# Sixteen modulation chunks of layer 1 move from layer 0's attention into layer 1's own stages

## The chip, the cores and the metric

One core of one Trainium2 chip runs the whole kernel in one launch. The metric is the device time in microseconds; three runs of the kernel before gave 1990.22, 1991.87 and 1993.07 us, and 1991.87 is their median. Engines are called by their names in the profile: PE is TensorE (PEld its weight loads), DVE VectorE, ACT ScalarE, POOL GpSimd, and SP the engine that issues most DMAs.

## The reference, cut to what matters

Two blocks run one after the other on 256 tokens of width 1024 (and 256 context tokens). The first block has two layers. Each computes, for a vector c and for the context's vector:

```
mod = silu(c) @ w_mod[l] + b_mod[l]            # 6 * 1024 values
sh1, sc1, gt1, sh2, sc2, gt2 = split(mod, 6)
proj = (rms_norm(x, g1) * (1 + sc1) + sh1) @ w_in
o_mla, o_gqa = attention(proj), attention(proj);  o_four = fourier_mix(proj)
x = x + gt1 * merge_branches(o_mla, o_gqa, o_four, gates)
x = x + gt2 * conv_ffn(rms_norm(x, g2) * (1 + sc2) + sh2)
```

sh1 and sc1 are wanted at the start of a layer, the other four from its merge on. Layer 0 also updates the context (four tiles of 128 rows, queries of the two context tiles see 256 keys, the others 512); layer 1 updates only the two token tiles, all with 512 keys. The second block (another mixer pair) is not touched.

## The kernel before, in words

Every engine has its program written out by hand; they meet by semaphores that count up. Products are made from two or three passes over split values (coarse and fine parts). Weights come through a ring of RING = 2 raw slots in SBUF, filled by SP in one fixed order (`load`, `chunks`, `stream`; L2898 is its DMA), each slot after the user of its last content has released it. For most weights ACT makes the coarse part (L1137) and DVE the fine one (L1839) before PE multiplies.

The modulation is cut into chunks of 256 columns, 24 for each layer. A chunk takes one raw slot (1 MB of w_mod) and is used unsplit: `mod_product` (L538) multiplies its eight rows of blocks in four strips of a bank, DVE copies the 98 rows out (`mod_row`, L1891), PE turns them with two transposes (L474), and DVE adds the strips and the bias into `mod_t` (L1871, L1872). `mod_chunk` of each engine does the second half of the chunk before and the first half of the next. The first eight chunks of layer 0 are made at the start. The other 16 of layer 0 and all 24 of layer 1 are made in layer 0: one in each of the eight tiles of `heads_prep`, and 32 in the attention's `heads_loop`, at the heads i listed in MOD_FILLS, which are the odd ones; `mod_chunk(last=True)` finishes the last one.

In `heads_prep`, for each tile PE makes the next tile's latent products (L527), then the chunk, then the transposes of the heads (L474); ACT squares and takes roots, DVE sums, scales and rotates (L2063 to L2088 for rotated tiles), and the transposes wait for it. In `heads_loop` the turn i has the score of head i (L693), the transposes of the exponentials of head i - 2 (L700), on even i the products with the values for heads i - 4 and i - 3 (L710), and then the fill. DVE takes the maximum (L2164, L2167), ACT the exp (L1402) and the copy of the turned exponentials (L1411), for which L710 waits.

Then `fourier` (L741, L751) runs over four groups for each pair of tiles, eight in layer 0 and four in layer 1. In its turn j = 2, in layer 0, `gate_transposes` turns the gate values (gt1 and gt2) of both layers into rows, and DVE's `other_gains` copies them out (L1821) to `gate_rows`, makes the three mod_gain products that are left (L1907) and raises mod_ready to 2. POOL waits for that, writes the rows to DRAM (L2818) and waits until they have landed; it reads them back, spread over partitions, for the merge's end and the FFN's end of each layer (L2825). ACT waits for the same landing ahead of `merge`, since its sigmoids (L1460) go to a buffer that lies over `gate_rows`; ACT's splits of the merge's weights stand behind that wait. In `merge` each slot carries 18 blocks of weights, the first slot is split during `fourier`, the second one inside the merge.

Of the kernel before, what the change touches and what calls it, by code (L numbers as in the profile page):

```python
# [13 lines left out]
P = 128  # L14
D = 1024
KD = D // P
SEQ = 256
DEPTH = 2
# [66 lines left out]
MOD_FILLS = [16 * t + i for t in range(4) for i in range(1, 16, 2)]  # L85
# [116 lines left out]
def two_block_kernel(nc, a, out):  # L202
    ctx = ExitStack()
    with ctx:
# [101 lines left out]
        gate_rows = rows(2 * KD, X + 17024, 512)  # L306
# [102 lines left out]
        def _(pe):  # L409
# [157 lines left out]
            def mod_chunk(last=False):  # L567

                if mod_copied:
                    pe.wait_ge(bank_read[mod_copied[-1][0]], mod_copied[-1][1])  # L570
                    transposes([mod_row[:, m * P:(m + 1) * P] for m in range(2)], parts_in=MOD_ROWS)
                if not last:
# [61 lines left out]
            def heads_prep(l):  # L634
# [18 lines left out]
                for s, (kind, t) in enumerate(tiles):  # L653
                    copied = following
                    if s + 1 < len(tiles):
                        following = products(*tiles[s + 1])
                    if l == 0:
                        mod_chunk()
                    mla_transposes(kind, t, raw[s % 2], copied)
                    gqa_transposes(kind, t)  # L660

            def attend(l):
# [17 lines left out]
                heads_loop(16 * items_of(l), score, value, pr, prT, keys_of, exp_done, mod_chunk, MOD_FILLS if l == 0 else (), sums_t)  # L680
# [39 lines left out]
            def gate_transposes(reads):  # L720

                evacuated(reads)
                ps = begin()
                for l in range(DEPTH):
                    for use, sec in enumerate((2, 5)):
                        blk = mod_t[:, l, sec * KD:(sec + 1) * KD, :].rearrange("p k s -> p (k s)")
                        j = 2 * l + use
                        mm = nc.tensor.transpose(ps[0:2 * KD, j * P:(j + 1) * P], blk, ident[:, :])
                end(mm)
# [142 lines left out]
            for l in range(DEPTH):  # L872
                norm(4, project=True, started=int(l == 0))
                project(l)
                latents(l)
                heads_prep(l)
                attend(l)
                if l == 0:
                    mod_chunk(last=True)
                    reads = list(u.reads)  # L880
                fourier(l, (lambda: gate_transposes(reads)) if l == 0 else None)
                merge(l)
                mix_out(l)
                norm(items_of(l))
                ffn_up(l)
                ffn_down(l)
# [194 lines left out]
        def _(act):  # L1081
# [74 lines left out]
            def mod_chunk(last=False):  # L1156
                if mod_chunks[0]:
                    skip()
                if not last:
                    ring.next()  # L1160
                    skip()
                    mod_chunks[0] += 1
# [20 lines left out]
            def norm(l, second, nt, updates):  # L1183
# [5 lines left out]
                act.wait_ge(mod_ready, 1 if l == second == 0 else 2)  # L1189
# [102 lines left out]
            def heads_prep(l):  # L1292
# [75 lines left out]
                for s, (kind, t) in enumerate(tiles):  # L1368
# [4 lines left out]
                    if l == 0:  # L1373
                        mod_chunk()
# [3 lines left out]
            def attend(l):  # L1378
# [3 lines left out]
                def after(g, b, n):  # L1382
# [5 lines left out]
                           MOD_FILLS if l == 0 else (), after, True)  # L1388
# [54 lines left out]
            def merge(l):  # L1443
                n = items_of(l) * P
                act.wait_ge(gates_saved, 16)
# [94 lines left out]
            for l in range(DEPTH):  # L1540
# [6 lines left out]
                if l == 0:  # L1547
                    mod_chunk(last=True)
                fourier(l, skip if l == 0 else None)
# [225 lines left out]
        def _(dve):  # L1775
# [98 lines left out]
            filled, noted = [FIRST_MOD], [FIRST_MOD]  # L1874

            def mod_units(last=False):

                units = [later()] if noted[0] > FIRST_MOD else []
                noted[0] += 1
                return units if last else units + [later()]  # L1880

            def mod_chunk(units=None, last=False):

                units = units or mod_units(last)
                if filled[0] > FIRST_MOD:
                    mod_out(units[0], *divmod(filled[0] - 1, MOD_CHUNKS), 1)
                if not last:
# [5 lines left out]
            def other_gains(reads):  # L1893

                copy_out(gate_rows, 2 * KD)
# [146 lines left out]
            def heads_prep(l):  # L2042
# [54 lines left out]
                for s, (kind, t) in enumerate(tiles):  # L2097
# [4 lines left out]
                    chunk = mod_units() if l == 0 else None  # L2102
# [30 lines left out]
                    if chunk:  # L2133
                        mod_chunk(chunk)
# [3 lines left out]
            def attend(l):  # L2138
                def after(g, b, ps):
                    if g >= 2:  # L2140
# [4 lines left out]
                           mod_chunk, MOD_FILLS if l == 0 else (), after, True)  # L2145
# [230 lines left out]
            for l in range(DEPTH):  # L2376
# [7 lines left out]
                if l == 0:  # L2384
                    mod_chunk(last=True)
                    reads = list(u.reads)
                fourier(l, (lambda: other_gains(reads)) if l == 0 else None)
# [324 lines left out]
        def _(pool):  # L2712
# [66 lines left out]
            for l in range(DEPTH):  # L2779
# [36 lines left out]
                if l == 0:  # L2816
# [65 lines left out]
        def _(sp):  # L2882
# [48 lines left out]
            for l in range(DEPTH):  # L2931
# [7 lines left out]
                if l == 0:  # L2939
# [114 lines left out]
```

## Time and profile before

| what | value |
|---|---|
| median of 3 runs | 1991.87 us |
| span of the profiled execution | 1988.9 us |
| PE busy | 1877.4 us (94%) |
| DVE, ACT, POOL busy | 1162.5, 933.1, 198.5 us |
| mean granted clock of PE | 0.983 |
| w_mod DMAs | 48 of 1024 KB |
| layer 0: preparation from its first chunk, attention, Fourier | from 151.9, 198.0, 342.1 us |
| layer 1: attention, Fourier, merge | from 1081.3, 1160.0, 1169.7 us |

The profiled execution has no other time than its span, from the first to the last instruction; the median of the timed runs is 3.0 us above it. The stage times are starts of PE's instructions in the timeline. A busy PE counts its pipelined matmuls to their modelled ends, so it can show as fully busy where the next matmul merely follows without a wait.

### The profile page before, as it was taken

Reading aid. Unit: us, or ns where it says so; the run is one execution under the profiler, and the core shown is the slowest. Engines: PE = TensorE matmul, PEld = TensorE weight load, DVE = VectorE, ACT = ScalarE, POOL = GpSimd, SP = SyncE. Lnnn points to the kernel's source line nnn. Section 1 sums busy time; section 2 is a strip of 40 time slices with the busy share of each in tenths; the row PEclk is TensorE's granted clock in tenths of the full one; section 3 lists DMA queues with packets and bytes.
Section 4 is the critical chain, followed back from the end, with each engine's and each line's share of the span. In section 5 each row is a group of like instructions: output and inputs, shape, how many; then the busy total and the mean of one; then the engine's idle time right before and its main releaser. Section 6 shows DMA issues by size and latency. Waiting matters only on the chain.

```text
span 1988.9 us, 31268 instructions
## 1 busy us (share of the span) xinstructions
PE 1877.4 (94%) x12063; PEld 1571.9 (79%) x12063; DVE 1162.5 (58%) x1802; ACT 933.1 (47%) x1427; POOL 198.5 (10%) x203
## 2 busy tenths in 40 slices
PE   5999999999998999999998889989999999899997
PEld 2875565788887888888784579989989888799996
DVE  3326566444346555523535456677744578789987
ACT  3327555323324333311436654455534656387782
POOL 4010001000011223210100000023301000100000
PEclk9999999999998999999998999989999999999999
DMA  9225668333332232232250036645557433444442
GB/s 310 91 80 169 197 221 273 97 95 95 90 110 81 89 102 94 96 116 95 85 170 6 1 88 177 191 143 181 178 190 217 158 118 104 150 151 146 146 137 101
DMA packets 262855, 265.36 MB, mean 133 GB/s; under 512 B 6342, under 2 KB 230960, under 8 KB 262752
## 3 DMA queue, kind: packets, MB, share of 16 engines
q1 hardware_dynamic: 257856, 249.32, 40.4%
q0 software_dynamic: 4448, 13.49, 2.2%
q8 instruction: 71, 1.16, 0.3%
q10 hardware_dynamic: 448, 1.12, 0.2%
q14 instruction: 32, 0.26, 0.0%
HBM read 262.81 MB, written 1.10 MB: 133 GB/s over the span
## 4 chain that ended last, share of the span: by engine, by line
PE 78%; DVE 12%; ACT 5%; DMA 2%; issue 2%; SPq 0%; DVEq 0%; ACTq 0%
PE bank L480 21%; PE bank L481 21%; PE bank L482 21%; PE bank L693 4%; DVE weights_fine L1839 2%; PE bank L710 2%; DMA region<-in_w_mod 2%; PE bank L538 2%; PE bank L474 2%; PE bank L527 2%; PE bank L700 1%; ACT weights_coarse L1137 1%; DVE region L2482 1%; DVE small L2164 1%; PE bank L950 0%
## 5 line engine op out<-in xcount | busy, mean ns | idle before, releaser
L1839 DVE TENSOR_TENSOR weights_fine<-region,weights_coarse 128x2048 fp32r<-128x2048 f32 (+2 forms) x181 | 417.7, 2308 | 346.8 <-ACT weights_coarse L1137 345.7
L1137 ACT CAST weights_coarse<-region 128x2048 fp32r<-128x2048 f32 (+3 forms) x185 | 355.0, 1919 | 333.0 <-PE bank L482 323.9
L480 PE MATMUL bank<-normed_coarse,weights_coarse 128*128 128x256 f32 (+1 forms) x1104 | 371.3, 336 | 9.2 <-DVE normed_fine L1977 4.3
L481 PE MATMUL bank<-normed_fine,weights_coarse 128*128 128x256 f32 (+1 forms) x1104 | 370.9, 336 | 0.0
L482 PE MATMUL bank<-normed_coarse,weights_fine 128*128 128x256 f32 (+1 forms) x1104 | 370.8, 336 | 0.0
L480 PEld LDWEIGHTS bank<-normed_coarse,weights_coarse 128*128 128x128 f32 x1104 | 212.4, 192 | 30.7 <-issue 10.1
L481 PEld LDWEIGHTS bank<-normed_fine,weights_coarse 128*128 128x128 f32 x1104 | 212.3, 192 | 20.5
L482 PEld LDWEIGHTS bank<-normed_coarse,weights_fine 128*128 128x128 f32 x1104 | 212.3, 192 | 20.4
L480 PE MATMUL bank<-x_turned_coarse,weights_coarse 128*128 128x256 f32 x616 | 177.8, 289 | 8.7 <-DVE weights_fine L1839 4.2
L481 PE MATMUL bank<-x_turned_fine,weights_coarse 128*128 128x256 f32 x616 | 175.5, 285 | 0.0
L482 PE MATMUL bank<-x_turned_coarse,weights_fine 128*128 128x256 f32 x616 | 175.5, 285 | 0.0
L1479 ACT ACTIVATE region<-bank,cols 128x512 f32<-128x512 f32 (+1 forms) x88 | 59.1, 672 | 216.4 <-PE bank L482 216.4
L480 PEld LDWEIGHTS bank<-x_turned_coarse,weights_coarse 128*128 128x128 f32 x616 | 119.4, 194 | 12.5 <-DVE weights_fine L1839 5.4
L2277 DVE SCALAR_TENSOR_TENSOR region<-bank,cols,region 128x510 f32<-128x510 f32 (+1 forms) x88 | 54.0, 614 | 114.0 <-ACT region L1479 113.0
L481 PEld LDWEIGHTS bank<-x_turned_fine,weights_coarse 128*128 128x128 f32 x616 | 119.5, 194 | 0.0
L482 PEld LDWEIGHTS bank<-x_turned_coarse,weights_fine 128*128 128x128 f32 x616 | 119.4, 194 | 0.0
L1402 ACT ACTIVATE region<-bank,small,q_scale 128x512 f32<-128x512 f32 (+1 forms) x96 | 67.9, 707 | 95.6 <-DVE small L2167 91.4
L693 PE MATMUL bank<-region 96*128 96x512 f32 (+4 forms) x224 | 106.6, 563 | 3.6 <-ACT region L1353 1.5
L480 PE MATMUL bank<-weights_coarse,ffn_mid_coarse 128*128 128x512 f32 x264 | 102.8, 389 | 0.9 <-DVE region L2243 0.9
L481 PE MATMUL bank<-weights_fine,ffn_mid_coarse 128*128 128x512 f32 x264 | 102.7, 389 | 0.0
L482 PE MATMUL bank<-weights_coarse,ffn_mid_fine 128*128 128x512 f32 x264 | 102.7, 389 | 0.0
L474 PE MATMUL bank<-ident,region 128*128 128x128 f32 (+3 forms) x449 | 69.0, 285 | 32.9 <-DMA ident<-in_c_ident 7.6
(295 smaller groups left out, 3574.4 us busy)
## 6 DMA issues: line engine op xcount, KB each, us to landing
region<-in_w_mod SPq DMA_DIRECT2D x48, 1024.0 KB, 5.3
region<-in_w_up SPq DMA_DIRECT2D x44, 1024.0 KB, 5.1
region<-in_w_in_c SPq DMA_DIRECT2D x30, 1024.0 KB, 5.2
region<-in_w_in_ab SPq DMA_DIRECT2D x20, 1024.0 KB, 5.3
region<-in_w_in SPq DMA_DIRECT2D x32, 512.0 KB, 4.7
region<-in_w_down SPq DMA_DIRECT2D x16, 1024.0 KB, 5.0
region<-in_w_in SPq DMA_DIRECT2D x14, 1024.0 KB, 5.0
region<-in_w_in SPq DMA_DIRECT2D x16, 384.0 KB, 3.5
```

Source lines behind the costliest of these rows:

```text
L474: mm = nc.tensor.transpose(ps[0:w, j * width:j * width + parts_in], blk, ident[0:parts_in, 0:parts_in])
L480: nc.tensor.matmul(o, sc, mc, start=first, stop=False)
L481: nc.tensor.matmul(o, sc, mf, start=False, stop=False)
L482: return nc.tensor.matmul(o, sf, mc, start=False, stop=last)
L527: mm = nc.tensor.matmul(ps[:, 0:n], acts[:, k, t * P:(t + 1) * P], w[:, k, c0:c0 + n], start=(k == 0), stop=(k == k_rows - 1))
L538: mm = nc.tensor.matmul(ps[strip:strip + 2, 0:COLS], sil_c[:, k, :], w[:, k, :], start=(k < MOD_STRIPS), stop=(k >= KD - MOD_STRIPS))
L693: nc.tensor.matmul(pb[4 + J % 2][:, 0:keys_of(i)[1] * P], q, k, start=True, stop=True).then_inc(scores_done, 1)
L1137: nc.scalar.copy(w_co[:, p, 0:size], raw_w[:, s, 0:size]).then_inc(coarse_ready, 1)
L1402: nc.scalar.activation(p_sb[:, J % 2, 0:nk], src, ACT.Exp, bias=small[:, at + J % 4:at + 1 + J % 4], scale=q_scale[:, i // 16, i % 16:i % ...
L1479: nc.scalar.activation(acc[:, j, 0:n], ps[:, 0:n], ACT.Identity, scale=cols[:, 2 * l, bass.ds(c + T_TAP1, 1)], bias=cols[:, 2 * l + 1, bas ...
L1839: nc.vector.tensor_tensor(w_fi[:, p, 0:size], raw_w[:, s, 0:size], w_co[:, p, 0:size].bitcast(F32), ALU.subtract).then_inc(fine_ready, 1)
L2277: link(nc.vector.scalar_tensor_tensor(out=a_s[:, :, 1:SEQ], in0=u_s[:, :, 0:SEQ - 1], scalar=cols[:, 2 * l, bass.ds(f + T_TAP0, 1)], in1=a ...
```

## The change

MOD_FILLS becomes a list for each layer. Layer 0's attention keeps 16 fills (the heads 1, 5, 9, 13 of each of its four tiles), which with the eight of its preparation finish layer 0 and make the first eight chunks of layer 1 (sh1 and sc1). Layer 1's other 16 chunks are made in layer 1: six in its preparation, ten in its attention. SP's order of loads follows. The gate transposes, the gate rows, their write to DRAM and the waits for it are done once in each layer, each for its own layer; mod_gain is made for layer 0's second norm and layer 1's first in layer 0, and for layer 1's second norm in layer 1. The number of chunks stays 48. The core of the diff:

```diff
-MOD_FILLS = [16 * t + i for t in range(4) for i in range(1, 16, 2)]
+MOD_FILLS = [[16 * t + i for t in range(4) for i in range(1, 16, 4)],
+             [16 * t + i for t in range(2) for i in (1, 5, 7, 11, 13)]]
...
-        gate_rows = rows(2 * KD, X + 17024, 512)
+        gate_rows = rows(2 * KD, X + 17024, 2 * P)
...  PE, ACT and DVE, heads_prep
-                    if l == 0:
-                        mod_chunk()
+                    mod_chunk()
...
-            def gate_transposes(reads):
+            def gate_transposes(l, reads):
 
                 evacuated(reads)
                 ps = begin()
-                for l in range(DEPTH):
-                    for use, sec in enumerate((2, 5)):
+                for use, sec in enumerate((2, 5)):
...  PE, ACT and DVE, the layers' loop
-                if l == 0:
-                    mod_chunk(last=True)
-                    reads = list(u.reads)
-                fourier(l, (lambda: gate_transposes(reads)) if l == 0 else None)
+                mod_chunk(last=True)
+                reads = list(u.reads)
+                fourier(l, lambda: gate_transposes(l, reads))
...  ACT
-                act.wait_ge(mod_ready, 1 if l == second == 0 else 2)
+                act.wait_ge(mod_ready, 1 if l == second == 0 else 2 + l * second)
...
-                act.wait_ge(gates_saved, 16)
+                act.wait_ge(gates_saved, 16 * (l + 1))
...  DVE
-            def other_gains(reads):
+            def other_gains(l, reads):
 
-                copy_out(gate_rows, 2 * KD)
+                copy_out(gate_rows, 2 * KD, 2 * P)
...
-                for layer, second in ((0, 1), (1, 0)):
-                    step(gains(layer, second))
-                gains(1, 1).then_inc(mod_ready, 1)
+                if l < DEPTH - 1:
+                    step(gains(l + 1, 0))
+                gains(l, 1).then_inc(mod_ready, 1)
...  POOL
-                if l == 0:
-                    pool.wait_ge(mod_ready, 2)
-                    pool.dma_start(gate_dram.rearrange("c r n -> r c n"),
-                                   gate_rows.rearrange("r (c n) -> r c n", c=2 * DEPTH)).then_inc(gates_saved, 16)
-                    pool.wait_ge(gates_saved, 16)
+                pool.wait_ge(mod_ready, l + 2)
+                pool.dma_start(gate_dram[2 * l:2 * l + 2].rearrange("c r n -> r c n"),
+                               gate_rows.rearrange("r (c n) -> r c n", c=2)).then_inc(gates_saved, 16)
+                pool.wait_ge(gates_saved, 16 * (l + 1))
...  SP
-                if l == 0:
-                    chunks(w_mod[0], FIRST_MOD * COLS, MOD)
-                    for later in range(1, DEPTH):
-                        chunks(w_mod[later], 0, MOD)
+                chunks(w_mod[l], FIRST_MOD * COLS, MOD)
+                if l < DEPTH - 1:
+                    chunks(w_mod[l + 1], 0, FIRST_MOD * COLS)
```

## Rows read from the trace of the kernel before

**Rows 1.** The page: its span, and the chain that ended last by engine.

```profile
span 1988.9 us, 31268 instructions
...
PE 78%; DVE 12%; ACT 5%; DMA 2%; issue 2%; SPq 0%; DVEq 0%; ACTq 0%
```

**Rows 2.** Waits of PE, layer 0's attention: us in total, times, longest.

```profile
PE bank L538 <- DMA region<-in_w_mod: 1.0, 2, 0.6
```

**Rows 3.** Timeline of PE, layer 0's attention, 512 keys: start, duration, instructions, [idle before].

```profile
220.93 0.33 PE L474 MATMUL bank<-ident,region 98*128 98x98 f32 x2
...
222.17 1.12 PE L693 MATMUL bank<-region 128*128 128x512 f32 x2
```

**Rows 4.** Timeline of PE, layer 1's attention.

```profile
1105.45 1.09 PE L710 MATMUL bank<-region 128*64 128x128 f32 x16 [0.62 <-ACT region L1411]
```

**Rows 5.** Timeline of PE, the end of layer 0's attention, 256 keys.

```profile
333.53 0.70 PE L693 MATMUL bank<-region 128*128 128x256 f32 x2
...
336.37 0.66 PE L710 MATMUL bank<-region 128*64 128x128 f32 x8
336.96 0.70 PE L693 MATMUL bank<-region 128*128 128x256 f32 x2
...
339.32 0.66 PE L710 MATMUL bank<-region 128*64 128x128 f32 x8
```

**Rows 6.** Timeline, head preparation of layer 0 and of layer 1.

```profile
154.81 1.19 PE L474 MATMUL bank<-ident,region 128*96 128x128 f32 x9 [1.90 <-DVE region L2129]
...
178.48 1.51 PE L474 MATMUL bank<-ident,region 128*96 128x128 f32 x12
...
183.27 0.42 DVE L2088 TENSOR_TENSOR region<-region 128x256 f32<-128x256 f32 x1
...
1052.95 1.19 PE L474 MATMUL bank<-ident,region 128*96 128x128 f32 x9 [2.84 <-DVE region L2129]
...
1072.44 1.04 PE L474 MATMUL bank<-ident,region 128*96 128x128 f32 x8
...
1078.88 1.11 PE L474 MATMUL bank<-ident,region 128*128 128x128 f32 x4 [0.92 <-DVE region L2088]
...
1081.26 3.78 PE L693 MATMUL bank<-region 96*128 96x512 f32 x4 [1.27 <-ACT region L1351]
```

**Rows 7.** Windows: busy time of each engine, then PEclk, DMA share and GB/s.

```profile
198.60:201.80 3.20, 3.20 (x9) 1.15 (x10) 1.01 (x3) 1.52 (x3) 0.77 (x1) 0.52 0.20 44
1079.00:1089.00 10.00, 8.48 (x16) 3.82 (x17) 2.55 (x6) 4.86 (x9) 0.74 (x1) 0.50 0.11 28
978.00:983.20 5.20, 5.20 (x25) 5.20 (x26) 4.42 (x9) 1.43 (x4) 0.00 (x0) 0.50 0.31 126
```

**Rows 8.** Timeline of layer 0's Fourier stage, and DMA issues (KB, us to landing).

```profile
342.06 1.93 PE L741 MATMUL bank<-region 128*128 128x258 f32 x8
...
351.54 0.67 DVE L1821 COPY region<-bank 16x512 f32<-16x512 f32 x1
...
352.98 0.54 POOL L2818 DMA_DIRECT2D gate_rows<-region  x1 [8.20 <-DVE mod_gain L1907]
...
gate_rows<-region POOLq DMA_DIRECT2D x1, 32.0 KB, 4.7
...
out<-x_tok SPq DMA_DIRECT2D x4, 256.0 KB, 2.1
```

**Rows 9.** Timeline of layer 1's Fourier stage and the merge's first turn.

```profile
1160.04 1.91 PE L741 MATMUL bank<-region 128*128 128x258 f32 x8
...
1167.52 1.28 ACT L1137 ACT_TABLE_LOAD   x1
1168.82 2.12 ACT L1137 CAST weights_coarse<-region 128x2304 fp32r<-128x2304 f32 x1
...
1171.87 2.55 DVE L1839 TENSOR_TENSOR weights_fine<-region,weights_coarse 128x2304 fp32r<-128x2304 f32 x1
...
1177.78 0.28 PE L480 MATMUL bank<-normed_coarse,weights_coarse 128*128 128x256 f32 x1
```

More of the change, by code:

```diff
@@ L571, in mod_chunk @@
                     transposes([mod_row[:, m * P:(m + 1) * P] for m in range(2)], parts_in=MOD_ROWS)
-                if not last:
+                if last:
+                    mod_copied.clear()
+                else:
                     mod_product()
@@ L678, in value @@
                     return proj[:, kt, at:at + 64]
[L680 removed]
+                heads_loop(16 * items_of(l), score, value, pr, prT, keys_of, exp_done, mod_chunk, MOD_FILLS[l], sums_t)
             def heads_loop(heads, score, value, p_sb, pT_sb, keys_of, scores_read, fill, fills, sums):
@@ L1158, in mod_chunk @@
                     skip()
+                mod_chunks[0] = int(not last)
                 if not last:
@@ L1372, in heads_prep @@
                         squares_of(s + 1)
-                    if l == 0:
-                        mod_chunk()
+                    mod_chunk()
                     turned_mla(kind, t)
@@ L1546, in _ @@
                 attend(l)
-                if l == 0:
-                    mod_chunk(last=True)
-                fourier(l, skip if l == 0 else None)
+                mod_chunk(last=True)
+                fourier(l, skip)
                 merge(l)
@@ L1872, in mod_out @@
                 read(nc.vector.tensor_tensor(mod_t[:, l, at, :], mod_t[:, l, at, :], bias, ALU.add), b)
-            filled, noted = [FIRST_MOD], [FIRST_MOD]
+            filled, noted = [FIRST_MOD, False], [False]
             def mod_units(last=False):
-                units = [later()] if noted[0] > FIRST_MOD else []
-                noted[0] += 1
+                units = [later()] if noted[0] else []
+                noted[0] = not last
                 return units if last else units + [later()]
@@ L1884, in mod_chunk @@
                 units = units or mod_units(last)
-                if filled[0] > FIRST_MOD:
+                if filled[1]:
                     mod_out(units[0], *divmod(filled[0] - 1, MOD_CHUNKS), 1)
+                filled[1] = not last
                 if not last:
@@ L2101, in heads_prep @@
                         skip(2)
-                    chunk = mod_units() if l == 0 else None
+                    chunk = mod_units()
                     skip(2)
@@ L2132, in heads_prep @@
                         nc.vector.tensor_tensor(keys, src, over_heads(small[:, 72:74], GQA_KV, GQA_DIM), ALU.mult).then_inc(gqa_ready, 1)
-                    if chunk:
-                        mod_chunk(chunk)
+                    mod_chunk(chunk)
                     before = turning
@@ L2144, in attend @@
                 heads_loop(16 * items_of(l), lambda i: 512 if i < 32 else 256, o_raw, sums_t, None,
-                           mod_chunk, MOD_FILLS if l == 0 else (), after, True)
+                           mod_chunk, MOD_FILLS[l], after, True)
             def heads_loop(heads, keys_of, raw_o, sums, bias, fill, fills, after, scaled=False):
@@ L2383, in _ @@
                 attend(l)
[L2384 to L2387, printed above, removed]
+                mod_chunk(last=True)
+                reads = list(u.reads)
+                fourier(l, lambda: other_gains(l, reads))
                 merge(l)
```

10 lines of the change are left out of this document (3 added, 7 removed).

## The prediction

> **What bounds the kernel now.** I began with the page's span and its chain of waits: TensorE carries 78% of the chain [rows 1]. Only gaps and extra work on TensorE therefore count, and I read the timeline in the stages that the change touches. Layer 0's attention is full: each turn with a modulation chunk shows no wait between the operations of TensorE, so each chunk pushes the rest back [rows 3], and twice the chunk's DMA was late as well, 1.0 us in all [rows 2]. Layer 1's attention has no chunks and waits 0.62 us per pair of heads for ScalarE's copy [rows 4]. Layer 1's head preparation waits at its first tile (2.84 us) and at its last two stages (0.92 and 1.27 us) [rows 6]. The windows of the granted clock show 10 us at 0.50 (1.2 of 2.4 GHz) from the end of that preparation into the attention, and only 3.2 us at the same place of layer 0 [rows 7].
>
> **Out of layer 0's attention** go 16 of 32 fills, at i = 3, 7, 11, 15 of each tile. A fill is two transposes and 16 matmul records: 220.93 to 222.17 is 1.24 us [rows 3]. While heads have 512 keys (8 of the 16), its place becomes a wait of 0.62 us, as in layer 1 [rows 4]: 8 x (1.24 - 0.62) = 5.0 us.
> With 256 keys the trace has no pair without a fill, so I bound it. From the odd head's score (336.96) to the product that needs the copy behind it (339.32) the chain score, maximum, exp, copy takes 2.36 us [rows 5]. In a pair with a fill TensorE comes to that product only after 336.37 - 333.53 = 2.84 us [rows 5], so nothing waits. Without the fill it would come at 2.84 - 1.24 = 1.60 us and wait until 2.36: a fill is worth 2.84 - 2.36 = 0.48. The bounds are 0 (another engine paces) and 1.24 (no wait). The last fill (i = 63) is worth nothing: its product already stood at 2.36. So 7 x 0.48 = 3.4 us. Half the chunks also halve the stream from HBM, and the 1.0 us of late DMAs goes [rows 2]. Sum 9.4 us.
>
> **Layer 0's Fourier stage** keeps its gate transposes, for one layer: the copy of the gate rows is 16x256 where it was 16x512 (0.67 us, [rows 8]), some 0.25 us less, and one gain product of three goes. TensorE waits for that copy's bank; I take 0.3 us. Sum for layer 0: 9.7 us saved.
>
> **Into layer 1's head preparation** go 6 chunks. I follow layer 0, which has the same first five tiles with chunks. From the first to the fifth set of MLA transposes layer 0 takes 178.48 - 154.81 = 23.67 us, layer 1 takes 1072.44 - 1052.95 = 19.49 [rows 6]: +4.18. The first tile's chunk falls into the 2.84 us wait and is free. The last tile is paced by VectorE's rotation, not by TensorE: in layer 0 the last rotate of the sixth tile ends at 183.27 + 0.42 = 183.69, the transposes behind it could start at 183.75, and layer 1 needs 1081.26 - 1078.88 = 2.38 us from there to its first score [rows 6]. That is 183.75 + 2.38 - 178.48 = 7.65 us from the fifth set on, against 1081.26 - 1072.44 = 8.82 now: -1.17, because the next tile's sums begin earlier against TensorE. Preparation: +3.0 us. Six full chunks (7.4) and 2 are the ends.
>
> **Into layer 1's attention** go 10 fills at odd i, the last at 29. Nine stand in the steady turns at 1.24 - 0.62 = 0.62 us: 5.6 us. The one at i = 1 stands in the stretch at the low clock. Its own price is 1.24; with chunks at the end of the preparation TensorE has fewer gaps, and the cold stretch should come nearer layer 0's 3.2 us than 10 [rows 7]. Half the clock for 6.8 us less is at most 3.4; I take half of it, 1.7, so this place gives -0.5. The ends are -2.2 (all 3.4) and +1.9 (no shorter, and the chunk itself half hidden at twice its price).
>
> The Trainium skill, TensorE: Matmul & The Clock Gate, section "HAM oscillation — how this bites in real kernels", says that gaps in TensorE's work put its clock to half rate and that each return is paid again, so that keeping it fed pays. Here the trace agrees in kind, 0.50 after gaps [rows 7]. It speaks for layer 1 as the home of the chunks; carried through, it is the first rival.
>
> **The seam behind layer 1's attention** is new. SP now puts w_mod chunks ahead of the first merge weights, which had been in their slots since the projection. They are loaded once the fills at i = 27 and 29 are done, with three pairs of heads still to come before the Fourier stage; in layer 0 the last fill has none behind it, and nothing waits for the weights there: hidden. The closing mod_chunk adds two transposes, 0.2 us.
> Then ScalarE may not enter the merge before the gate rows of its own layer are in DRAM, since the sigmoids write over them. Behind that wait on ScalarE stand the split of the second weight slot, VectorE's half of it, and then TensorE. I count from the stage's first matmul (342.06 in layer 0, 1160.04 in layer 1). In layer 0 the copy starts at +9.48, POOL's DMA at +10.92, and it lands 4.7 us later [rows 8]. In layer 1 the same order holds up to there (both wait for ScalarE's 2304-wide split and VectorE's); a narrower copy and one gain instead of three give +10.5, landing +15.2. Table load 1.28, cast 2.12, VectorE 2.55 [rows 9] bring TensorE's second slot to +21.3. It starts at 1177.78, +17.74, now [rows 9]. That is 3.6 us, 3.8 with the transposes. TensorE comes to it about when it does now, so it stands still for 3 us or more; layer 0 hides the same chain because it has eight Fourier groups, not four. The ends: the shortest write to DRAM in the trace lands in 2.1 us [rows 8], which makes it 1.2; a landing two microseconds later than layer 0's makes it 6.
> Cold stretches behind gaps of TensorE are 3.2 us long in the short kind and 5.2 in the longer [rows 7]; half of that is lost, 1.6 or 2.6 us. I take 1.7; 0 and 2.6 are the ends. Layer 1's merge waits for nothing that could give this back.
> DMA: Bandwidth & Descriptors of the Trainium skill, section "Anatomy of one DMA — SWDGE (gpsimd) path", has some 2 us fixed for such a DMA. The trace has 4.7 with the weights' stream running beside it; by the page's figure the seam would cost about 1.1 and hardly any cold time. The measured one stands in the sum.
> POOL has only the gate loads behind its two waits, and these wait for the merge's end anyway. The norms' wait on mod_ready is met long before.
>
> **Sum.** Layer 1: 3.0 + 5.6 - 0.5 + 3.8 + 1.7 = 13.6 us. Layer 0: -9.7. Net +3.9 us. On the profiled span of 1988.9 us that is 1992.8; the median of the runs is 1991.87, 3.0 above that span, so I forecast 1995.8 us. A change of 0.2%, 4.0 us, is about what can be told from none; the forecast lies on that line.
>
> **Rivals.**
> Fed TensorE (the other side). Chunks close the gaps at the end of the preparation, the attention starts in a short cold stretch or none (another 1.7 us back) and the stall in the merge brings no cold time (1.7 less): +3.9 - 3.4 = +0.5, 1992.4, not slower by what can be told. For it: layer 0's 3.2 us. Against it: the rotation still paces the last tile, and TensorE keeps gaps there. It decides once the cold stretch at the start of the attention falls to layer 0's length and the merge stays at full clock.
> Short gate write. It lands in 2.1 us as the output's writes do [rows 8], 2.6 sooner, and the merge's stall is too short for a cold stretch: +3.9 - 2.6 - 1.7 = -0.4, 1991.5. Against it: SP's four issues of the next slot stand at the same place in both layers.
> Colder still. The cold stretch stays at 10 us with the chunk of i = 1 in it (+1.9 for -0.5), and the stall is paid with 5.2 us at half: +3.9 + 2.4 + 0.9 = +7.2, 1999.1.
> The saving does not come. Another engine paces layer 0's 256-key heads, and the late DMAs were part of the same wait: 4.4 us less saved, 2000.2. Against it: in the tail of that attention, with the fill out of the way, the chain itself took 2.36 us [rows 5].
>
> **How the numbers follow.** Forecast 0.56, with its own range 1993.3 to 1998.3; fed TensorE 0.16; short write 0.11; colder 0.11; no saving 0.06. Slower by over 0.2% (above 1995.9): half the forecast's case and the last two: 0.45. Faster by over 0.2% (below 1987.9) needs the first two rivals together and more: 0.07. Within: 0.48. The range that takes in the rivals' centres: 1989.8 to 2000.4.
>
> **What would show it.** Sixteen fills with 0.48 to 0.62 us waits in place of them in layer 0; a pair without fill at 256 keys lasting 2.95 us; layer 1's first score 3.0 us later against the first tile; a table load on ScalarE about 15 us after layer 1's first Fourier matmul, released by the gate write; a TensorE gap of 3 to 5 us before the second slot and 0.50 clock after it. I am wrong if the gate write lands before +12, if the cold stretch before the attention is gone, or if layer 0's pairs keep their length.

## The result and the profile after

The changed kernel takes 2002.26 us in the median of five runs (2001.82 to 2003.16), the kernel before 1991.93 (1990.22 to 1993.07, five runs of the same job). The ratio is 1.0043, with a 95% interval of 1.0031 to 1.0056: 8.6 us slower (6.2 to 11.2 by the interval, which holds the 10.3 us between the two medians). In a later job the changed kernel took 2003.13 and the ratio was 1.0037 (1.0020 to 1.0054). The forecast was 1995.8 with a range up to 2000.4, so it is outside, on the slow side.

The page of the profiled run (2003.16 us, span 2001.3) has the same chain as before [rows 1]:

```profile
span 2001.3 us, 31252 instructions
...
PE 79%; DVE 12%; ACT 5%; issue 2%; DMA 2%; SPq 0%; DVEq 0%; ACTq 0%
```

The difference must be read by stage. The table has the length of each stretch, from one TensorE start to the next, less the same stretch of the profile before; a plus is time lost. "Seam" is layer 1's Fourier stage and merge, up to the output mix; "behind" is all that follows, where the change alters no instruction. The last two columns are a second profile of the changed kernel and one of the kernel before.

| stretch, us | forecast | changed | changed again | before again |
|---|---|---|---|---|
| layer 0 attention | -9.4 | -7.71 | -8.70 | -0.52 |
| layer 0 Fourier | -0.3 | +0.28 | -0.36 | +1.32 |
| layer 1 preparation | +3.0 | +3.21 | +3.21 | 0.00 |
| layer 1 attention | +5.1 | +4.83 | +4.83 | 0.00 |
| layer 1 seam | +5.5 | +7.06 | +7.02 | -0.01 |
| behind | 0 | +4.39 | +4.40 | +0.06 |

**Layer 0's attention.** The timeline of TensorE at the end of it (start, duration, instructions, [idle before]), which answers to [rows 5]:

```profile
326.36 0.66 PE L712 MATMUL bank<-region 128*64 128x128 f32 x8 [0.95 <-ACT region L1409]
...
329.79 0.66 PE L712 MATMUL bank<-region 128*64 128x128 f32 x8
...
332.74 0.66 PE L712 MATMUL bank<-region 128*64 128x128 f32 x8 [0.94 <-ACT region L1409]
```

A pair with a fill lasts 329.79 - 326.36 = 3.43 us, one without 332.74 - 329.79 = 2.95, which is the length forecast. At 512 keys the wait in place of a fill is 0.62, as forecast:

```profile
219.24 1.09 PE L712 MATMUL bank<-region 128*64 128x128 f32 x16 [0.62 <-ACT region L1409]
```

The waits of TensorE in this attention hold no late w_mod chunk any more [rows 2]; ScalarE's copy took its place (us in total, times, longest):

```profile
PE bank L712 <- ACT region L1409: 12.5, 17, 1.0
```

What is missing from the 9.4 us is at the end. Windows of the changed kernel, first the end of layer 0's attention, then the start of layer 1's, which was 10 us at 0.50 [rows 7] (busy time of PE, PEld, DVE, ACT, POOL, then PEclk, DMA share, GB/s):

```profile
334.00:338.50 4.50, 4.28 (x21) 3.62 (x22) 1.53 (x5) 1.10 (x3) 0.70 (x1) 0.62 0.10 24
...
1077.50:1082.00 4.50, 4.50 (x22) 1.48 (x22) 1.95 (x6) 2.69 (x5) 0.75 (x1) 0.62 0.21 59
```

The second window holds about 3.4 us of half clock (4.50 us at 0.62), as much as layer 0's start of attention has [rows 7]. The second profile of the same kernel has the first of these windows at full clock, and there the attention saves 8.70:

```profile
334.00:338.50 4.50, 4.36 (x28) 3.60 (x26) 1.10 (x4) 3.00 (x4) 1.27 (x1) 1.00 0.02 4
```

**The seam.** All engines, layer 1's Fourier stage and the merge's first turn, in the changed kernel; it answers to [rows 9]. The first Fourier matmul starts at 1161.02:

```profile
1168.02 2.55 DVE L1836 TENSOR_TENSOR weights_fine<-region,weights_coarse 128x2304 fp32r<-128x2304 f32 x1
...
1170.49 0.41 DVE L1818 COPY region<-bank 16x256 f32<-16x256 f32 x1
...
1170.60 2.24 SPq L2893 DMA_DIRECT2D region<-in_w_in  x3
...
1171.58 0.55 POOL L2813 DMA_DIRECT2D gate_rows<-region  x1 [7.84 <-DVE mod_gain L1905]
...
1176.81 1.28 ACT L1136 ACT_TABLE_LOAD   x1 [5.88 <-DMA gate_rows<-region]
...
1178.10 2.11 ACT L1136 CAST weights_coarse<-region 128x2304 fp32r<-128x2304 f32 x1
...
1180.25 2.56 DVE L1836 TENSOR_TENSOR weights_fine<-region,weights_coarse 128x2304 fp32r<-128x2304 f32 x1 [6.57 <-ACT weights_coarse L1136]
...
1182.94 0.58 PE L481 MATMUL bank<-normed_coarse,weights_coarse 128*128 128x256 f32 x1 [5.97 <-DVE weights_fine L1836]
...
1187.97 0.28 PE L481 MATMUL bank<-branch_out,weights_coarse 128*128 128x256 f32 x1
```

VectorE's half of the first slot is done, its buffer is free, and SP sends three DMAs for the next slot; 0.98 us behind them POOL sends the 16 KB of gate rows. The write starts at +10.56 (forecast +10.5), the table load at +15.8 (+15.2), and TensorE takes up the work behind the second slot's split at +21.92 (+21.3). It stood still for 5.97 us and then ran at half clock:

```profile
1180.50:1188.00 7.50, 5.06 (x25) 5.07 (x26) 3.54 (x2) 3.79 (x4) 0.00 (x0) 0.54 0.59 151
```

To say how much later that is, the same matmul must be found in the kernel before. In `merge` the wait for the second slot stands behind the first two gates, that is behind 2 x 8 blocks or 48 matmuls, since the third gate takes its blocks from both slots. Windows of the first 48 matmuls of the merge, before and changed:

```profile
1169.70:1177.05 7.35, 7.34 (x48) 7.34 (x49) 4.58 (x9) 2.90 (x3) 0.00 (x0) 0.77 0.83 204
```

```profile
1170.94:1177.00 6.06, 6.01 (x48) 5.81 (x48) 2.43 (x9) 0.19 (x1) 0.55 (x1) 1.00 0.77 197
```

So the 49th is the one to compare, and before it ran at 1177.06, +17.02; the 1177.78 (+17.74) of [rows 9] is the 55th, six matmuls behind the wait. TensorE of the kernel before:

```profile
1177.06 0.28 PE L480 MATMUL bank<-normed_coarse,weights_coarse 128*128 128x256 f32 x1
...
1179.94 0.28 PE L480 MATMUL bank<-branch_out,weights_coarse 128*128 128x256 f32 x1
```

The wait therefore costs 21.92 - 17.02 = 4.90 us. From there to the first matmul on the branches the same 24 matmuls take 1187.97 - 1182.94 = 5.03 us, mostly at half clock, where they took 1179.94 - 1177.06 = 2.88, so 2.15 us go to the clock. The two make up the seam's 7.06.

**Behind the seam.** Windows from the first matmul of layer 1's output mix to the end, before and changed:

```profile
1274.98:1988.90 713.92, 675.42 (x5106) 626.58 (x5104) 531.80 (x724) 406.77 (x538) 65.14 (x66) 0.98 0.48 153
```

```profile
1283.02:2001.30 718.28, 679.21 (x5106) 630.74 (x5104) 532.47 (x724) 407.16 (x538) 65.19 (x66) 0.98 0.47 152
```

The same 5106 matmuls keep TensorE busy for 3.79 us longer, and its waits grow by only 0.57: what is lost there is mostly clock, not waiting. The clearest place is the second block, where nothing was changed. TensorE waits 2.80 us for the same split of weights in both kernels. The kernel before, timeline and window:

```profile
1633.17 0.39 PE L480 MATMUL bank<-x_turned_coarse,weights_coarse 128*128 128x256 f32 x1 [2.80 <-DVE weights_fine L1839]
```

```profile
1633.00:1639.00 6.00, 5.83 (x48) 5.83 (x49) 6.00 (x11) 3.81 (x5) 0.00 (x0) 1.00 0.58 175
```

The changed kernel:

```profile
1642.49 0.58 PE L481 MATMUL bank<-x_turned_coarse,weights_coarse 128*128 128x256 f32 x1 [2.80 <-DVE weights_fine L1836]
```

```profile
1642.40:1649.00 6.60, 6.51 (x32) 6.51 (x33) 6.60 (x11) 3.83 (x5) 0.00 (x0) 0.54 0.54 159
```

The gap is equal; the clock behind it is 2.4 GHz in one and mostly 1.2 in the other. That stretch, from the second block's attention to its mix, is 2.59 us longer, in both profiles of the changed kernel.

### The profile page after: what moved, and what is told of

It is laid out like the page before. It is cut to its first block, busy times and chain, and to the rows that moved or that the text cites. A ratio compares the mean times of both kernels' runs of the same rounds, so it can differ in the third digit from the quotient of the medians.

```text
span 2001.3 us, 31252 instructions
## 1 busy us (share of the span) xinstructions
PE 1883.8 (94%) x12063; PEld 1578.2 (79%) x12063; DVE 1159.7 (58%) x1803; ACT 933.9 (47%) x1427; POOL 199.1 (10%) x204
## 4 chain that ended last, share of the span: by engine, by line
PE 79%; DVE 12%; ACT 5%; issue 2%; DMA 2%; SPq 0%; DVEq 0%; ACTq 0%
PE bank L481 21%; PE bank L483 21%; PE bank L482 21%; PE bank L695 4%; PE bank L712 2%; DVE weights_fine L1836 2%; PE bank L528 2%; PE bank L475 2%; PE bank L539 2%; DMA region<-in_w_mod 1%; ACT weights_coarse L1136 1%; PE bank L702 1%; DVE region L2478 1%; PE bank L949 1%; DVE small L2161 1%
```

## The experiments

Medians and ratios are against the kernel before in the same job; its median was 1993.4 to 1996.2 in these jobs. Here are the stretches of each kernel's profile, less those of the profile before, in us.

| kernel | median us | ratio (95%) | L0 attention | L1 prep + attention | seam | behind |
|---|---|---|---|---|---|---|
| rows_apart | 1994.09 | 1.0010 (0.9995-1.0025) | -8.68 | +8.03 | -0.86 | +2.17 |
| gates_only | 2005.43 | 1.0063 (1.0049-1.0077) | -0.65 | +0.75 | +7.14 | +5.40 |
| gates_again | 2007.33, one run | | -0.29 | -0.07 | +7.65 | +6.10 |
| thin0 | 1985.73 | 0.9960 (0.9944-0.9976) | -8.61 | +0.03 | +0.01 | -0.04 |
| extra1 | 2003.66 | 1.0052 (1.0038-1.0066) | -0.11 | +8.03 | -0.02 | +1.86 |
| early_rows | 1997.21 | 1.0016 (1.0005-1.0027) | -8.70 | +8.93 | -0.75 | +5.83 |
| placed | 1991.60 | 0.9991 (0.9981-1.0001) | +0.12 | +1.61 | -1.24 | +4.45 |
| wait_only | 2003.58 | 1.0034 (1.0020-1.0048) | +0.93 | +0.03 | +5.29 | +1.60 |
| gates_apart | 1993.31 | 0.9987 (0.9972-1.0001) | -0.71 | -0.09 | +0.22 | +1.31 |
| hold_stream | 2002.63 | 1.0037 (1.0025-1.0048) | -8.68 | +8.02 | +3.22 | +5.81 |

**Moving the chunks alone.** thin0 is the kernel before without layer 1's last sixteen chunks; layer 1's modulation values are set to zero, so that part is left out.

```
-MOD_FILLS = [16 * t + i for t in range(4) for i in range(1, 16, 2)]
+MOD_FILLS = [16 * t + i for t in range(4) for i in range(1, 16, 4)]
...
-    chunks(w_mod[later], 0, MOD)
+    chunks(w_mod[later], 0, FIRST_MOD * COLS)
...
+    link(nc.vector.memset(mod_t[:, 1, :, :], 0.0))
```

> The kernel before without the last 16 chunks of layer 1 (left out altogether, their part of the modulation stays zero); layer 0's attention has 16 fills. My sum: 9.4 us less in layer 0's attention; the trace of the changed kernel has 7.7, with a stretch at half clock at the attention's end. Expect 1982.5 to 1984.5 by the sum, 1984.5 by the trace. Rival (other stages take back what the thinner attention gives, by the clock): 1987 or more.

extra1 does the opposite: the chunks stay in layer 0, and layer 1 works its sixteen again in its own stages, with the gates of both layers still in layer 0.

```
+    [16 * t + i for t in range(2) for i in (1, 5, 7, 11, 13)]   # layer 1, beside the 32 fills of layer 0
...  SP, so once more in layer 1
+    chunks(w_mod[l], FIRST_MOD * COLS, MOD)
```

> The kernel before, and layer 1's last 16 chunks computed once more in layer 1's preparation and attention (six and ten, as in the change); gates and rows as before. My sum: +3.0 in the preparation, +5.1 at the attention: about 2000.0; the changed kernel's trace shows +3.2, -1.2 and +6.1, so 2000.0 as well. Rival (each chunk costs its full 1.24 us): +20, 2012. Rival (the slots taken by chunks make the merge's first weights late): more than 2003, with a DMA wait at the merge.

Without the sixteen, layer 0's attention is 8.6 us shorter and the kernel 0.40% faster (8.0 us). With them in layer 1, its preparation and attention are 3.22 + 4.81 = 8.03 us longer. The measured 10.4 us (1.0052) is about these 8.0 and 1.9 behind the seam. Both kernels came out above their expectations, thin0 by 1 to 3 us and extra1 by 3.7; the kernel before had a median 1.5 above its first one in that job. Sixteen chunks are worth 8 to 9 us in either layer; the move by itself brings nothing. It also shows the head preparation (+3.2) and the attention (+4.8) apart from every other edit.

**The gates alone.** gates_only has the chunks where they were and only the gates by layer, with the wait at each merge; gates_again is the same kernel a second time.

```
-    pool.dma_start(gate_dram.rearrange(...), gate_rows.rearrange("r (c n) -> r c n", c=2 * DEPTH))
+    pool.wait_ge(mod_ready, l + 2)
+    pool.dma_start(gate_dram[2 * l:2 * l + 2].rearrange(...), gate_rows.rearrange("r (c n) -> r c n", c=2))
...
-    act.wait_ge(gates_saved, 16)
+    act.wait_ge(gates_saved, 16 * (l + 1))
```

> The kernel before with its 40 chunks in layer 0, but gate transposes, gate rows and their write once per layer, as in the change. Seam theory: the seam alone costs 6 to 7 us in layer 1, of which 0.3 us comes back in layer 0: about 1998. Rival (the seam is late only because the chunks fill the queue ahead of the merge's weights): about 1992 to 1993.

The gates alone carry the loss: 1.0063, and the seam is 7.1 us longer with no chunk moved. The seam came as expected, the total did not: 2005.43 for about 1998, with 5.4 us behind the seam. The wait and the gap stand as in the changed kernel; TensorE of gates_only:

```profile
1182.99 0.57 PE L480 MATMUL bank<-normed_coarse,weights_coarse 128*128 128x256 f32 x1 [6.07 <-DVE weights_fine L1839]
```

**The wait taken away.** rows_apart is the changed kernel with the gate rows in the place of `mod_row`, which is free by then, so that the sigmoids do not write over them and ScalarE need not wait.

```
-gate_rows = rows(2 * KD, X + 17024, 2 * P)
+gate_rows = rows(2 * KD, X + 24192, 2 * P)
...
-act.wait_ge(gates_saved, 16 * (l + 1))
```

> The changed kernel, with the gate rows in the place of mod_row (free by then) and no wait for their write ahead of the merge on ScalarE. Seam theory (the write's landing holds ScalarE's second split and with it TensorE for 6 us, and the cold clock comes behind): 6 to 7 us faster than the changed kernel, about 1995.5, layer 1's merge starts its second slot within 0.5 us of the first slot's end, no stretch at half clock there. Rival (TensorE would have waited for weights from the ring all the same, which now come later): under 2 us faster, about 2001, with a wait for a w_in or w_four DMA in the seam. Rival (the loss is spread over untouched stages): about 2000 and stages of the second block as in the changed kernel.

The table load follows at once, and the merge runs at full clock (timeline of ScalarE, window):

```profile
1169.10 1.28 ACT L1136 ACT_TABLE_LOAD   x1
```

```profile
1169.00:1177.00 8.00, 7.79 (x62) 7.59 (x63) 5.04 (x11) 6.29 (x7) 0.55 (x1) 1.00 0.66 161
```

The seam goes from +7.06 to -0.86: 7.9 us, more than the 5.5 forecast for it. A part of it is below the level of the kernel before, whose own merge had a stretch at low clock with TensorE busy without a break:

```profile
1170.00:1175.00 5.00, 5.00 (x31) 5.00 (x31) 4.30 (x7) 1.68 (x2) 0.00 (x0) 0.66 0.91 231
```

5.00 x 0.34 = 1.7 us are lost there in the kernel before and none in rows_apart.

gates_apart is gates_only with the same two lines changed.

```
-gate_rows = rows(2 * KD, X + 17024, 2 * P)
+gate_rows = rows(2 * KD, X + 24192, 2 * P)
...
-act.wait_ge(gates_saved, 16 * (l + 1))
```

> gates_only with the gate rows in memory of their own and ScalarE's wait for the gate write gone: chunks placed as in the kernel before, gates per layer, no wait at the merge. Seam theory: the 7 us are gone and the merge is 0 to 1.5 us shorter than before, as in rows_apart (-1.1). Alignment theory: the stages from the mix on are longer than before by 2 to 5 us although nothing waits, as in rows_apart, so the profiled time is 1988.9 - 1 + 3 = 1991 and the median within 0.2% of before. Rival (the downstream loss needs the stall in the merge): those stages as before within 0.5 us, 1988.

Per-layer gates without the wait cost nothing at the seam (+0.22), and the ratio is 0.9987 (0.9972 to 1.0001). Behind the seam it has +1.31, where one theory had 2 to 5 us and its rival at most 0.5; that decides for neither. At the seam it is settled: neither the transposes nor the narrower copies cost anything.

**The wait put in.** wait_only is the kernel before, where layer 1's ScalarE waits for a write of 16 KB that nobody reads; it has no gate transposes in layer 1 and no moved chunk.

```
+more_rows = rows(2 * KD, X + 24192, 2 * P)
...
+step(nc.vector.memset(more_rows, 0.0)); step(gains(1, 0)); gains(1, 1).then_inc(mod_ready, 1)
...
+pool.wait_ge(mod_ready, 3)
+pool.dma_start(more_dram.rearrange(...), more_rows.rearrange(...)).then_inc(gates_saved, 16)
...
-act.wait_ge(gates_saved, 16)
+act.wait_ge(gates_saved, 16 * (l + 1))
```

> The kernel before with one thing of the seam alone: in layer 1's Fourier stage VectorE sets a 16x256 piece of memory and works two gain products again, POOL writes that piece to a DRAM tensor of its own that nobody reads, and ScalarE waits for it ahead of layer 1's merge. No gate transposes in layer 1, no chunk moved, the layer-0 gates as before; all that is computed is as before. Seam theory (the wait alone costs it): 5 to 8 us between the first merge matmul of layer 1 and the output mix, as in the changed kernel (6.8) and in gates_only (6.9, 7.4). Rival (the narrower gate rows and the transposes carry a part of it): 0 to 3 us. For the stages behind the seam, alignment theory: a TensorE whose merge of layer 1 runs otherwise meets the later gaps otherwise, so the mix to the end is some 2 to 6 us longer here too, 1988.9 + 7 + 4 = 2000 profiled. Code theory (only the per-layer gates bring it): those stages stay within 0.3 us in sum of before, 1996 profiled.

The seam is 5.29 longer: the wait alone costs that. Behind it stand +1.60, less than the 2 to 6 expected and more than the rival's 0.3. ScalarE and TensorE of wait_only:

```profile
1182.39 1.28 ACT L1139 ACT_TABLE_LOAD   x1 [7.21 <-DMA more_rows<-region]
...
1188.44 0.39 PE L482 MATMUL bank<-normed_coarse,weights_coarse 128*128 128x256 f32 x1 [3.56 <-DVE weights_fine L1841]
```

The gap is 3.56 us and not 5.97 for two reasons. Its TensorE spent part of the first slot at the lower clock (0.72 over the first 6.0 us of the merge), as the kernel before does (1170 to 1175, above), and came to the second one 1.5 us later; and its table load came 1.1 us earlier, at +14.7 for +15.8. In the changed kernel the first slot runs at full clock (1172 to 1176, below), straight into the wait.

**Why the write lands late.** early_rows gives VectorE the gate copy ahead of the split of the first slot.

```
 if j == 2:
+    if among:
+        among()
     fine(SLOT)
-if among and j == 2:
-    among()
```

> The changed kernel, with the gate rows copied out and sent by VectorE before its fine part of the merge's first slot instead of behind it (2.55 us earlier). Seam theory: the gate write starts near +8 after the Fourier stage's first matmul, lands near +13, the second slot starts near +19.3 instead of +21.9; TensorE's gap is 3.4 to 4 us instead of 6; 2.5 us faster than the changed kernel, more (4) where the cold stretch goes too: about 1999.5. Rival (the write lands at a fixed time set by the weights' stream): no change in the seam, 2002.

POOL issues at +8.09 instead of +10.56, and the write lands sooner by more than that. POOL, SP and ScalarE of early_rows:

```profile
1172.46 0.54 POOL L2813 DMA_DIRECT2D gate_rows<-region  x1 [5.37 <-DVE mod_gain L1905]
...
1174.41 1.28 ACT L1136 ACT_TABLE_LOAD   x1 [1.46 <-DMA gate_rows<-region]
...
1174.66 2.22 SPq L2893 DMA_DIRECT2D region<-in_w_in  x3
```

1.95 us from issue to ScalarE instead of 5.23, because SP's stream now starts behind it. The seam is 7.8 us shorter than in the changed kernel, where 2.5 to 4 were expected. But this moves two things at once, the order and the time.

hold_stream changes only the stream: SP waits for the gate write before it sends the slot.

```
 def merge_pieces(i, j):
+    if l == 1 and j == 2 and type(i) is int:
+        sp.wait_ge(gates_saved, 32)
```

> The changed kernel with one wait added on SP: in layer 1 it issues the merge's third weight slot (three DMAs, 1170.60 in the changed kernel) only when the gate write has landed, so that POOL's write at 1171.58 runs with no stream beside it. All is computed as before. Stream theory (the write lands late because the weights' 278 to 288 GB/s go through the same DMA engines): issue to ScalarE's table load falls from 5.2 to about 2 us, as in early_rows (1172.46 to 1174.41), TensorE's gap of 5.97 falls to about 3, the merge is 3.0 us shorter, or 4.5 where the cold stretch goes too: 6.8 becomes 2.3 to 3.8, median 1998 to 2000. The third slot lands some 4.3 us after 1173.6, ahead of its cast. Rival (the write is slow of itself in that place, 5 us, and the stream moves behind it): the merge stays at 6.8 or gets longer by the late third slot, median 2002 or more.

DMA issues around the seam (KB, us from issue to landing), first the changed kernel, then hold_stream:

```profile
gate_rows<-region POOLq DMA_DIRECT2D x1, 16.0 KB, 5.0
```

```profile
gate_rows<-region POOLq DMA_DIRECT2D x1, 16.0 KB, 1.7
```

Windows of the changed kernel while the write is under way, the last two columns being the DMA share and GB/s:

```profile
1172.00:1174.00 2.00, 2.00 (x19) 2.00 (x18) 1.57 (x6) 0.00 (x0) 0.13 (x1) 1.00 0.98 278
1174.00:1176.00 2.00, 2.00 (x19) 2.00 (x19) 0.00 (x0) 0.00 (x0) 0.00 (x0) 1.00 1.14 288
1176.00:1178.00 2.00, 0.97 (x9) 0.76 (x7) 0.00 (x0) 1.19 (x1) 0.00 (x0) 1.00 0.06 16
```

The write lands when the stream ends. With the stream held, ScalarE and TensorE read:

```profile
1171.94 1.28 ACT L1136 ACT_TABLE_LOAD   x1 [2.63 <-DMA gate_rows<-region]
...
1178.08 0.38 PE L481 MATMUL bank<-normed_coarse,weights_coarse 128*128 128x256 f32 x1 [2.71 <-DVE weights_fine L1836]
```

The gap is 3.26 us shorter and the seam 3.84 (+3.22 for +7.06): in the rows the stream theory held. The median did not show it: 1.0037 against 1.0043 and 1.0037 of the changed kernel, with intervals that overlap; 1.4 us of it are given back behind the seam in the profile (+5.81 for +4.39). Its runs span 1999.13 to 2006.71, and the profiled one is the fastest of them. The expected 1998 to 2000 was missed, so the stream is shown by the rows of one profile and not by the time.

**The stages behind.** Three kernels were profiled a second time.

> The kernel before, unchanged, profiled once more. Clock-phase theory (whether a short gap of TensorE is followed by half clock depends on when it falls, not on the kernel's text): the stages up to the modulation's first use and the gap of 2.8 us ahead of the second block's output product come out 1 to 3 us different, the span between 1989 and 1998. Rival (the kernel fixes where the clock falls): the same cold stretches at the same places, span 1988 to 1990.

> gates_only, unchanged, profiled once more. Seam theory: layer 1's merge again about 6.9 us longer than in the kernel before. Clock-phase theory: its 3 us at the start of the second block and 1.4 us after its attention are not all there again. Rival: every stage within 0.3 us of the first profile of gates_only.

after_again is the changed kernel.

> The changed kernel once more, profiled a second time. Settled-by-the-kernel theory: each kernel has its own places of half clock behind the seam, so the stages from the output mix of layer 1 to the end are again 4 us longer than before in sum, the merge again 6 to 7.5 longer, profiled 2000 to 2003. Rival (the places of half clock are drawn anew in each execution): the touched stages are the same within 0.3 us each, while the stages behind the seam sum to anything between 0 and 6 us over before, and the runs of this kernel spread over some 8 us as those of the others did, against 1.3 us in its first five runs.

Behind the seam the second profile differs from the first by 0.06 us (before), 0.01 (changed) and 0.70 (gates_only, of which 0.6 is in the output mix). So the places of half clock there belong to the kernel and are not drawn anew each time. Ahead of it they do vary: layer 0's attention and Fourier stage differ by 1.6 us between the two profiles of the changed kernel, and layer 0's Fourier stage alone by 1.3 between those of the kernel before. So behind the seam the rival of the clock-phase theory held; that theory fits only the stages ahead of it.

In gates_again one of these stretches follows no gap at all. TensorE ran through sixteen small matmuls on 32 rows and then had:

```profile
1557.10:1563.00 5.90, 5.90 (x29) 5.88 (x29) 2.77 (x2) 3.54 (x3) 0.00 (x0) 0.51 0.08 11
```

**A better placing.** placed is rows_apart with all 32 odd fills kept in layer 0's attention, one chunk instead of eight in its preparation, and seven chunks in layer 1.

```
+PREP_FILLS = [(0,), (0, 5)]
+MOD_FILLS = [[16 * t + i for t in range(4) for i in range(1, 16, 2)], [1, 7, 13, 19, 25]]
+SECOND_FROM = FIRST_MOD + 9
```

> rows_apart with the chunks placed where TensorE waits anyway: layer 0's preparation keeps one of eight (the first tile's, which falls into a wait), its attention has 32 fills, layer 1's preparation has two (first and last tile), its attention five; layer 1 makes 7 chunks. Price list from the traces: a chunk costs 1.24 us in the preparation, 0.5 to 0.6 in an attention, nothing in the first tile. Against rows_apart: -8.7 in layer 0's preparation, +8 to +9 in its attention, -3.2 in layer 1's preparation, -3.1 in its attention: 7 us faster, about 1987, 5 to 6 below the kernel before. Rival (the preparation is paced by VectorE or ScalarE once the chunks are gone): 4 us less of a gain, about 1991.

Layer 0's preparation fell by only 4.73 us where 8.7 were expected, 4 less, as the rival said. Waits of TensorE up to the attention's first score (us in total, times, longest), placed and then rows_apart:

```profile
PE bank L697 <- ACT region L1354: 3.6, 1, 3.6
PE bank L476 <- DVE region L2129: 2.3, 2, 1.9
```

```profile
PE bank L475 <- DVE region L2126: 1.9, 1, 1.9
```

Once the chunks are gone, TensorE waits for ScalarE and VectorE there, most of all ahead of the first score. Layer 1 grew by 1.61 and the seam fell by 1.24; 4.45 came back behind the seam. The ratio of 0.9991 (0.9981 to 1.0001) is no faster than before by what can be told. Nor is gates_apart.

## Why the prediction failed

The sign and the order of the terms were right, the size was not: 8.6 us slower by the ratio, 3.9 forecast. In the touched stages the terms sum to -7.43 + 3.21 + 4.83 + 7.06 = +7.7 (+6.0 in the second profile), where the forecast has +3.9. Two steps failed in both profiles: the seam's terms, forecast +5.5 and measured +7.06, and the stages behind it, put at nothing and measured +4.4. None of the three signs of being wrong came: the gate write landed behind +12, the cold stretch before layer 1's attention was shorter but there, and layer 0's pairs got shorter. None of them looked at the stages behind the seam.

- **Layer 0, forecast -9.7.** -7.43 in the first profile, -9.06 in the second. The parts held: 0.62 at 512 keys, a pair of 2.95 us at 256 keys, the late DMAs gone. What the sum lacked is that an attention with waits in it can end in a stretch at half clock (334.00:338.50, above); it did in one profile of two. Of the 0.7 us that the other lacks of 9.4, no row tells more than that the kernel before itself differs by 0.5 between its two profiles. The rival "the saving does not come" fell: thin0, rows_apart and the second profile have 8.6 to 8.7.
- **Layer 1's preparation, +3.0.** +3.21, shown alone by extra1 (+3.22). Layer 0 was a good model of layer 1.
- **Layer 1's attention, +5.6 - 0.5.** +6.07 from the first value product to the Fourier stage, which has the closing transposes too, and -1.24 ahead of it. The cold stretch did shrink, from 10 us at 0.50 to 4.5 at 0.62, which is about layer 0's length; with the chunk's own 1.24 it gave back 2.5 us, where 1.7 was taken and 3.4 was the most.
- **The seam, +3.8 + 1.7.** The failed term of the touched part: +7.06, of which 4.90 is the wait and 2.15 the clock behind it. The forecast's 3.6 for the wait was counted from the wrong matmul: 1177.78 is six matmuls behind the place where TensorE waits, 1177.06. Its own +21.3 less +17.02 would have been 4.3; the other 0.6 is that the chain came at +21.92. The clock took 2.15 for 1.7, inside its ends of 0 and 2.6. wait_only (+5.29) and rows_apart (-0.86) show from both sides that the wait does it. The rival "short gate write" is a real state of the machine but not of this kernel: hold_stream and early_rows reach it, with 1.7 us to landing in the one and 1.95 us to ScalarE's table load in the other, and the price of it, 2.6 + 1.7 = 4.3 us, is near the 3.84 measured. The 2 us that DMA: Bandwidth & Descriptors of the Trainium skill gives for such a DMA ("Anatomy of one DMA — SWDGE (gpsimd) path") is what these two show with the queue empty; beside the stream the trace has 5.0, and it decides here.
- **The other rivals.** "Fed TensorE" fell: the start of the attention gave back more, as it said, but the merge did not stay at full clock. "Colder still" was nearest in its sum, +7.2, for a wrong reason in half of it: the stretch at the attention's start did not stay at 10 us.
- **Behind the seam, 0.** The step that failed most, since it is not in the sum at all: "Layer 1's merge waits for nothing that could give this back" was the end of the reckoning, and what lies behind was taken as unchanged. It is +4.39 and +4.40, 3.79 of it TensorE busy longer with the same matmuls. TensorE: Matmul & The Clock Gate of the Trainium skill ("HAM oscillation — how this bites in real kernels") lets the clock fall after gaps; the 2.80 us gap with full clock behind it in one kernel and half in the other shows that the gap's length alone does not tell.

What decides which of the later places turns cold stays open. It is 0.0 in thin0 and in the second profile before, the two kernels whose layer 1 is untouched, although thin0 comes there some 6 us earlier. It is 1.3 to 6.1 in the others, whether they have the wait (wait_only 1.60, gates_only 5.40), the moved chunks without it (rows_apart 2.17) or neither (gates_apart 1.31). That it needs the stall falls with placed (4.45, no stall); that it needs the gates' code falls with wait_only and extra1 (1.86).

The two profiles differ by 12.4 us in their spans: 7.7 in the touched stages, 4.4 behind, and 0.3 ahead of and between them (+2.1 and -1.7, where the two profiles of the changed kernel differ by 1.0 and 1.2). That the ratio of the runs gives 8.6 and not 12.4 no row here explains fully; the profile before is one of the fastest runs of its kernel, and the profiled run of the changed kernel the slowest of its five.

## What to carry to other kernels

A small write that an engine had to wait for landed here at the end of the stream that was issued just ahead of it: put such rows where nobody writes over them, so that nobody waits, or issue the write before a buffer's release starts the stream. Work of the same size moved between two stages with the same slack moves no time; look at the waits the move needs, not at the work. To size a new wait, find in the code which operation stands right behind it, and take that one's time from the trace. Leave room behind a changed stage: stages that were not touched got up to 6 us longer here by TensorE's clock, and the same again in a second profile, so a gain or loss of that size in one profile proves nothing about the edit.

## What was not expected of the hardware

- The 16 KB write from POOL took 5.0 us to land beside 278 to 288 GB/s of loads, and 1.7 with the stream held back.
- The same 2.80 us gap of TensorE was followed by full clock in one kernel and by 0.54 over 6.6 us in another, and each repeated in a second execution.
- TensorE was granted 0.66 over 5.00 us in which it was busy for 5.00 (layer 1's merge, before), and 0.51 over 5.90 of 5.90 (gates_again).
- The kernel before, unchanged, ran between 1989.9 and 2001.3 us in the later jobs, a spread larger than the effect that was asked for.
